# Last block of transposes without the output projection woven in (three causal layers), and four pairs of the mixed layer in two groups

## Chip, cores and metric

The kernel runs on one core of one Trainium2 chip. The metric is the device time of one execution in microseconds (us), from the start of the program to its end. A profiled execution also has a span, from its first to its last instruction.

## What is computed

Four layers of one block (MLA, sliding window "SWA", forgetting attention "FOX", MLA again), then one "mixed" layer with attention over heads of two kinds, a gated feed-forward part and a last gated projection. One sequence of 512 tokens, width 1024, everything in float32. Cut to what matters here:

```python
def first_block(x, ...):
    for i in range(DEPTH):                      # MLA, SWA, FOX, MLA
        y = branch(x)                           # (o * silu(gate)) @ w_out, o = causal softmax attention, 16 heads
        x = _layernorm(DEEPNORM_ALPHA * x + y, ln_g[i], ln_b[i])
    return x

def second_block(x, ...):
        z = rmsnorm(x, g_mix_pre[i]) @ w_in[i]
        ya = short_conv_mixer(a_in, a_c, a_b, conv_w[i])
        yb = pool_mixer(pv, pool_w[i], pool_scale[i])
        yc = dsa_mixer(...)                     # 4 heads, 128 keys of each query chosen by top-k, bias by distance
        yd = moba_mixer(...)                    # 4 heads, all past keys, bias by distance
        mix = jnp.concatenate([ya, yb, yc, yd], axis=-1) @ w_out[i]
        x = x + rmsnorm(mix, g_mix_post[i])
        f = swiglu(rmsnorm(x, g_ffn_pre[i]), w_gate_up[i], w_down[i])
        ...
```

## The kernel before

Every engine runs a program written out by hand, and semaphores tie them together. TensorE (PE) does all products. A float32 product is made of three fp32r products (high by high, high by low, low by high), so each weight that SyncE's queue brings in is split: ScalarE (ACT) copies the high part (`w_hi`, L1465), GpSimd (POOL) subtracts to get the low part (`w_lo`, L2992). A "unit" is one such weight piece. A **tile** is 24 matmuls of 128x512 for one unit of 128 columns (L545); its result lands in one of two PSUM banks, 6 and 7, ACT copies the high part out (L1494) and VectorE (DVE) the low part (L2182), which frees the bank. `three` (L496 to L498) is the same trick for the other products, the output projection `w_out` among them: one k-step of it has 24 matmuls, 6 for each of four rows of tokens.

Attention runs on **pairs** of heads. For a pair PE makes scores in three chunks (L735; for the chosen keys a further product L752 adds the mask of the top-k), DVE adds the bias and takes the maximum (L2334, "maxima"), ACT takes the exponential (L1596, "exps"), the result is divided by the sum, PE turns it by 20 transposes (L781, in 6 **turns** of 4, 4 and 2), ACT copies each turn out of PSUM (L1630), and PE multiplies by the values (L798, "mix", 16 matmuls).

In the causal layers (MLA, FOX, MLA) the division is DVE's (L2363), and the eight pairs go in four groups of two: `fill` (tiles and values for the next group), then a **block** of 12 turns on six banks, two mixes, and the scores of the next two pairs. The last group is different. `last_block` first calls `ahead(0)`, the first k-step of the output projection for two of its four rows, and then weaves two turns at a time between the products of `ahead(0)` to `ahead(2)`, 36 matmuls in all, and its turns have only two banks (4 and 5), since the projection holds 0 to 3:

```python
                    ahead(0)
                    two()
                    woven.append(each_second)
                    ahead(1)
                    ahead(2)
                    woven.pop()
                    while todo:
                        two()
```

In the mixed layer there are four pairs: 0 and 1 over all past keys, 2 and 3 over chosen keys. They are not grouped: `step` interleaves the turns of pair i with the scores of pair i+2, two banks for the turns, and tiles of queries and keys stand between them. Here ACT does the division (L1611), and DVE finds the chosen keys by 16 rounds of MAX8 and MATCH_REPLACE8 for each row of queries (L2803, L2804, `top`). The values of pairs 2 and 3 are made in two halves (L627), one before `mix(1)` and one before `mix(2)`, and ACT copies each half out (L1517). `mixed_ahead` then weaves the turns of pair 3 into the output projection.

## Time and profile before

| what | us |
|---|---|
| median of 3 runs | 1645.56 (1645.0 to 1646.14) |
| the profiled execution, its own time | 1647.99 |
| its span | 1645.8 |
| PE busy | 1626.4, 99% |
| DVE busy | 778.5, 47% |
| ACT busy | 763.9, 46% |

The span is 2.2 us below the profiled execution's own time, and within 0.3 us of the median of the runs. Times of day below are us from the start of the span. Matmuls overlap, so the time that a piece of PE's work takes is read from the start of its first instruction to the start of the next piece, not from the busy column.

### The profile page before, as it was taken

To read this page: it belongs to the slowest core of one execution; us is meant where nothing else is said; L and a number is where in the kernel's file an instruction comes from. 1 tells how busy PE (TensorE), PEld (TensorE's weight loads), DVE (VectorE), ACT (ScalarE), POOL (GpSimd) and SP (SyncE) were. 2 spreads that over 40 slices of the span, in tenths; PEclk is the share of its full clock that TensorE was granted. 3 is DMA by queue.
4 is the path that set the end of the run, shared out by engine and by line. 5 is a ranking of instruction groups with operands and counts; after the bars stand their busy time and mean duration, and the time that the engine had idled before them with its cause. 6 is when DMAs were issued, how large, how long until landed. Compare 5 with 4: busy or idle time off the path is not lost.

```text
span 1645.8 us, 24549 instructions
## 1 busy us (share of the span) xinstructions
PE 1626.4 (99%) x9349; PEld 1345.9 (82%) x9349; DVE 778.5 (47%) x2048; ACT 763.9 (46%) x1565; POOL 657.1 (40%) x551
## 2 busy tenths in 40 slices
PE   8999999999999999999999999999999999999998
PEld 8787879888888888778878788787788888888877
DVE  2787735665554433445878556896051111001152
ACT  4477634565344534633667534338553322212252
POOL 4423234332344224134333144882335444444423
PEclk9999999999999999999999999999999999999999
DMA  6322244323443223144232066241243333333312
GB/s 175 74 44 66 73 154 133 82 69 73 155 141 99 67 77 90 39 167 116 51 69 83 29 195 190 60 115 52 93 126 106 100 92 100 103 91 102 120 60 90
DMA packets 216048, 161.19 MB, mean 98 GB/s; under 512 B 53755, under 2 KB 197147, under 8 KB 215932
## 3 DMA queue, kind: packets, MB, share of 16 engines
q1 hardware_dynamic: 205904, 130.21, 28.1%
q10 hardware_dynamic: 9804, 29.38, 5.6%
q8 instruction: 75, 1.23, 0.3%
q14 instruction: 41, 0.34, 0.1%
q0 software_dynamic: 224, 0.03, 0.1%
HBM read 148.32 MB, written 11.14 MB: 97 GB/s over the span
## 4 chain that ended last, share of the span: by engine, by line
PE 88%; DVE 7%; ACT 2%; issue 1%; DMA 0%; ACTq 0%; POOL 0%; DVEq 0%; SPq 0%
PE banks L545 44%; PE banks L496 8%; PE banks L498 8%; PE banks L497 8%; PE banks L781 5%; PE banks L798 4%; PE banks L627 4%; PE banks L735 4%; PE banks L758 1%; DVE banks L2486 1%; DVE banks L2475 1%; DVE AB L2488 1%; ACT G L1743 1%; PE banks L1009 1%; DVE AB L2334 1%
## 5 line engine op out<-in xcount | busy, mean ns | idle before, releaser
L2992 POOL TENSOR_TENSOR w_lo<-w_raw,w_hi 128x512 fp32r<-128x512 f32 (+2 forms) x506 | 616.4, 1245 | 958.7 <-ACT w_hi L1465 947.7
L1465 ACT ACTIVATE w_hi<-w_raw 128x1024 fp32r<-128x1024 f32 (+4 forms) x254 | 250.2, 995 | 179.2 <-PE banks L498 107.2
L545 PE MATMUL banks<-XTh,w_hi 128*128 128x512 f32 (+5 forms) x1216 | 277.6, 370 | 1.7 <-DVE XTl L2448 1.4
L545 PE MATMUL banks<-XTl,w_hi 128*128 128x512 f32 (+5 forms) x1216 | 270.8, 365 | 0.0
L545 PE MATMUL banks<-XTh,w_lo 128*128 128x512 f32 (+5 forms) x1216 | 270.7, 365 | 0.0
L545 PEld LDWEIGHTS banks<-XTh,w_hi 128*128 128x128 f32 (+2 forms) x1216 | 208.2, 187 | 47.7 <-issue 8.2
L545 PEld LDWEIGHTS banks<-XTl,w_hi 128*128 128x128 f32 (+2 forms) x1216 | 211.0, 187 | 37.7
L545 PEld LDWEIGHTS banks<-XTh,w_lo 128*128 128x128 f32 (+2 forms) x1216 | 211.0, 187 | 37.4
L1596 ACT ACTIVATE AB<-AB,nb 128x256 f32<-128x256 f32 (+3 forms) x288 | 152.6, 533 | 37.7 <-DVE nb L2344 32.4
L496 PE MATMUL banks<-w_hi,OTh 128*128 128x512 f32 (+1 forms) x432 | 166.7, 386 | 0.3
L498 PE MATMUL banks<-w_hi,OTl 128*128 128x512 f32 (+1 forms) x432 | 162.4, 376 | 0.0
L497 PE MATMUL banks<-w_lo,OTh 128*128 128x512 f32 (+1 forms) x432 | 162.2, 375 | 0.0
L2363 DVE TENSOR_SCALAR_CACHE_REDUCE AB<-AB,ri 128x256 f32<-128x256 f32 (+3 forms) x256 | 118.2, 518 | 2.3
L1630 ACT ACTIVATE AB<-banks 128x512 f32<-128x512 f32 (+1 forms) x200 | 89.9, 566 | 37.0 <-PE banks L781 36.6
L2182 DVE TENSOR_TENSOR QKl<-banks,QKh 128x512 fp32r<-128x512 f32 (+2 forms) x80 | 54.6, 683 | 110.8 <-ACT QKh L1494 110.6
L2883 DVE TENSOR_TENSOR otmp<-banks,AB 128x512 f32<-128x512 f32 x22 | 15.2, 692 | 192.1 <-PE banks L545 192.1
L496 PEld LDWEIGHTS banks<-w_hi,OTh 128*128 128x128 f32 x432 | 81.7, 189 | 18.8 <-DVE QKl L2182 2.4
L498 PEld LDWEIGHTS banks<-w_hi,OTl 128*128 128x128 f32 x432 | 81.7, 189 | 15.0
L497 PEld LDWEIGHTS banks<-w_lo,OTh 128*128 128x128 f32 x432 | 81.7, 189 | 13.2
L1494 ACT ACTIVATE QKh<-banks 128x512 fp32r<-128x512 f32 (+2 forms) x80 | 46.9, 587 | 91.1 <-PE banks L545 67.3
L2334 DVE CUSTOM_DVE_ANT_0 AB<-banks,zmask 128x256 f32<-128x256 f32 (+1 forms) x192 | 81.5, 487 | 7.5 <-PE banks L758 5.2
L781 PE MATMUL banks<-ident,AB 128*128 128x128 f32 x672 | 83.2, 274 | 0.8
(232 smaller groups left out, 2265.6 us busy)
## 6 DMA issues: line engine op xcount, KB each, us to landing
w_raw<-in_w_gate_up_dram SPq DMA_DIRECT2D x44, 512.0 KB, 3.7
w_raw<-in_fox_w_in_dram SPq DMA_DIRECT2D x30, 512.0 KB, 4.1
w_raw<-in_mla_w_in_dram SPq DMA_DIRECT2D x26, 512.0 KB, 4.5
w_raw<-in_w_in_dram SPq DMA_DIRECT2D x24, 512.0 KB, 3.9
w_raw<-in_w_down_dram SPq DMA_DIRECT2D x22, 512.0 KB, 3.5
w_raw<-in_swa_w_in_dram SPq DMA_DIRECT2D x20, 512.0 KB, 4.0
w_raw<-in_mla_w_out_dram SPq DMA_DIRECT2D x16, 512.0 KB, 3.6
x_spill<-AB ACTq DMA_DIRECT2D x16, 512.0 KB, 2.8
```

The costliest lines, as they stand in the source:

```text
L496: nc.tensor.matmul(o, ah, bh, start=first, stop=False, skip_group_check=True)
L497: nc.tensor.matmul(o, ah, bl, start=False, stop=False, skip_group_check=True)
L498: return nc.tensor.matmul(o, al, bh, start=False, stop=last, skip_group_check=True)
L545: mm = nc.tensor.matmul(o, wt[:, k, :], xt[:, k, lo:hi], start=first and n == 0 and k == 0, stop=last and n == 2 and k == nk - 1, skip_gro ...
L627: mm = nc.tensor.matmul(o[:, 256 * (t % 2):256 * (t % 2) + 256], xt[:, k, ts], parts[k // 4][low][:, k % 4, :], start=n == 0 and k == 0, s ...
L781: mm = nc.tensor.transpose(turn_bank(m, grouped or six, block_at[1])[:, o:o + P], SBP[a % 2][x][:, col:col + P], ident[:, :])
L1465: nc.scalar.activation(view(w_hi, u, RING), view(w_raw, u, RAW), ACT.Copy).then_inc(hi_done, 1)
L1596: ins = nc.scalar.activation(sc, sc, ACT.Exp, bias=nb[:, b, n0 + t:n0 + t + 1], scale=pr.scale, accum_out=rs[:, b, n0 + t:n0 + t + 1])
L1630: nc.scalar.activation(dst[:, pr.pt[js[0]]:pr.pt[js[0]] + width], src[:, 0:width], ACT.Copy).then_inc(pt_free, 1)
L2334: ins = nc.vector.tensor_tensor_reduce(pr.score(b, x, t), o, pr.bias(t, x), 1.0, -3e38, ALU.add, ALU.max, mx[:, b, 4 * x + t:4 * x + t + 1])
L2363: ins = nc.vector.tensor_scalar(pr.score(b, x, t), pr.score(b, x, t), ri[:, b, 4 * x + t:4 * x + t + 1], None, ALU.mult, ALU.add, accum_ou ...
L2992: ins = pool.tensor_tensor(low[at], raw[at], high[at].bitcast(F32), ALU.subtract)
```

## The change

In the causal layers `pair_attention` is called with no `ahead`: all four groups run the same loop, the last one too, with its block of 12 turns on six banks, its two mixes, and then the whole output projection (`pairs=True` keeps its waits on single pairs). In the mixed layer the pairs become grouped: PE's order is the same loop as in the causal layers, and ACT and DVE get a new `scaled_groups`. SWA keeps `last_block`.

```diff
@@ PE, groups()
-                        last = s == n_pairs // 2 - 1
+                        last = s == n_pairs // 2 - 1 and ahead is not None
                         fill(s)
                         if last:
                             last_block(s)
...
-                        if not last:
-                            for i in (2 * s + 2, 2 * s + 3):
-                                for ch in range(s_len):
-                                    scores(i, ch)
+                        for i in (2 * s + 2, 2 * s + 3):
+                            for ch in range(s_len):
+                                scores(i, ch)
@@ PE, the three causal layers
-                pair_attention(mla_pairs(), fill, lambda k: out_ahead("out", src, k, each=True))
-                out_rows("out", KD, src, turned=(lambda t: HT[t % 2]) if j else (lambda t: x_tok[:, t, :]), 
+                pair_attention(mla_pairs(), fill, None)
+                out_rows("out", KD, src, pairs=True, turned=(lambda t: HT[t % 2]) if j else (lambda t: x_tok[:, t, :]), 
...
@@ PE, mixed layer
+            def fill(s):
+                if s < 0:
+                    pair_tile("q", 1)
+                    pooled(1)
+                    mark["mixed_g"] = c.g
+                    pair_tile("k", 1)
+                    pe.wait_ge(pool_out, 2)
+                elif s == 0:
+                    for p in (2, 3):
+                        pair_tile("q", p)
+                        pair_tile("k", p)
+                else:
+                    parts.extend([unit("v"), unit("v")])
+                    for half in range(2):
+                        value_half(parts, half)
...
+                    ready_pv[c.pair + 2] = c.g
@@ ACT
+                def scaled_groups():
+
+                    fill(-1, 0)
+                    for s in range(n_pairs // 2):
+                        for k in range(2):
+                            i = 2 * s + k
+                            exps(i, 0)
+                            exps(i, 1)
+                            fill(s, 2 * k)
+                            norm(i, 0)
+                            norm(i, 1)
+                            fill(s, 2 * k + 1)
+                        block_at[0] = c.tch
+                        turned(2 * s)
+                        turned(2 * s + 1)
+                        store(2 * s)
+                        store(2 * s + 1)
...
+                elif s == 0:
+                    pair_tile(2 + pos // 2 + pos % 2 * 4)
                 elif pos == 1:
-                    if i < 1:
-                        pair_tile(i + 7)
-                    elif i == 1:
-                        advance()
-                        values(0)
-                    elif i == 2:
-                        values(1)
-                elif pos == 5 and i == 2:
                     advance()
-
-            pair_attention(rel_pairs(), fill, (2,))
+                    values(0)
+                elif pos == 2:
+                    values(1)
+                    advance()
@@ DVE
+            def fill(s, pos):
+                if s < 0:
+                    top(3)
+                    pair_tile(1)
+                    pooled(1)
+                    top(2)
+                    pair_tile(5)
+                elif s == 0:
+                    pair_tile(2 + pos // 2 + pos % 2 * 4)
+                    top((3, 1, 3, 48)[pos])
```

Three places show the order. First PE at the end of the first MLA layer's attention, before the change: the last of the woven pieces (L496 to L498 the projection, L781 transposes, L798 the mixes).

```order
L781 MATMUL banks<-ident,AB 128x128 x8
L496 MATMUL banks<-w_hi,OTh 128x512
L497 MATMUL banks<-w_lo,OTh 128x512
L498 MATMUL banks<-w_hi,OTl 128x512
L496 MATMUL banks<-w_hi,OTh 128x512
L497 MATMUL banks<-w_lo,OTh 128x512
L498 MATMUL banks<-w_hi,OTl 128x512
L781 MATMUL banks<-ident,AB 128x128 x12
L798 MATMUL banks<-AB,V_odd 64x512 x2
```

The same place after the change, from the last gate tile (L545) on:

```order
L545 MATMUL banks<-XTl,w_hi 128x512 x8
L545 MATMUL banks<-XTh,w_lo 128x512 x8
L781 MATMUL banks<-ident,AB 128x128 x40
L798 MATMUL banks<-AB,V_odd 64x512 x2
L798 MATMUL banks<-AB,V_odd 64x384 x2
```

The 36 matmuls of the projection that stood before and between the transposes have moved behind the mixes.

Second, PE in the mixed layer before the change, at the end of pair 0's first two chunks of scores (L735), where the key tile of pair 1 follows:

```order
L735 MATMUL banks<-QKh 128x512 x2
L735 MATMUL banks<-QKl,QKh 128x512 x2
L735 MATMUL banks<-QKh,QKl 128x512 x2
L545 MATMUL banks<-XTh,w_hi 128x512 x8
L545 MATMUL banks<-XTl,w_hi 128x512 x8
```

and after it, where pair 0's last chunk of scores is followed by pair 1's first two:

```order
L735 MATMUL banks<-QKh 128x512 x2
L735 MATMUL banks<-QKl,QKh 128x512 x2
L735 MATMUL banks<-QKh,QKl 128x512 x2
L735 MATMUL banks<-QKh 128x256 x2
L735 MATMUL banks<-QKl,QKh 128x256 x2
L735 MATMUL banks<-QKh,QKl 128x256 x2
L735 MATMUL banks<-QKh 128x384 x2
```

The six chunks of pairs 0 and 1 now follow each other, and the four tiles of pairs 2 and 3 come behind them.

Third, ACT ahead of the turns of the mixed layer's second group, after the change (L1509 a half of the values, L1457 a weight split, L1603 the division, L1622 the copies of turns):

```order
L1509 ACTIVATE V<-banks 128x512
L1457 ACTIVATE w_hi<-w_raw 128x1024
L1603 ACTIVATE AB<-AB,ri 128x128
L1603 ACTIVATE AB<-AB,ri 128x256
L1603 ACTIVATE AB<-AB,ri 128x384
L1603 ACTIVATE AB<-AB,ri 128x512
L1603 ACTIVATE AB<-AB,ri 128x128
L1603 ACTIVATE AB<-AB,ri 128x256
L1603 ACTIVATE AB<-AB,ri 128x384
L1603 ACTIVATE AB<-AB,ri 128x512
L1622 ACTIVATE AB<-banks 128x512 x2
```

and before it (L1630 the copies, L1465 the split, L1611 the division):

```order
L1630 ACTIVATE AB<-banks 128x512 x2
L1630 ACTIVATE AB<-banks 128x256
L1465 ACTIVATE w_hi<-w_raw 128x1024
L1611 ACTIVATE AB<-AB,ri 128x128
L1611 ACTIVATE AB<-AB,ri 128x256
```

The first copy of pair 2's turns stood ahead of pair 3's division, and stands behind the whole of it now.

## Rows read from the trace of the kernel before

**Rows 1.** The page: span and the engines' busy time.

```profile
span 1645.8 us, 24549 instructions
PE 1626.4 (99%) x9349; PEld 1345.9 (82%) x9349; DVE 778.5 (47%) x2048; ACT 763.9 (46%) x1565; POOL 657.1 (40%) x551
```

**Rows 2.** Timeline of PE, first MLA layer, last group: start, length, line, operation, count.

```profile
196.82 0.39 PE L496 MATMUL banks<-w_hi,OTh 128*128 128x512 f32 x1
199.55 1.03 PE L781 MATMUL banks<-ident,AB 128*128 128x128 f32 x8
...
210.09 4.53 PE L798 MATMUL banks<-AB,V_odd 128*64 128x512 f32 x32
214.55 0.50 PE L496 MATMUL banks<-w_hi,OTh 128*128 128x512 f32 x1
```

**Rows 3.** Timeline of PE, the same layer's third group: block and mixes.

```profile
170.28 4.53 PE L781 MATMUL banks<-ident,AB 128*128 128x128 f32 x40
174.74 4.53 PE L798 MATMUL banks<-AB,V 128*64 128x512 f32 x32
```

**Rows 4.** Timeline of DVE, what follows the last division, MLA and FOX.

```profile
199.56 0.68 DVE L2215 SCALAR_TENSOR_TENSOR G<-G,banks 128x512 f32<-128x512 f32 x1
...
689.05 0.68 DVE L2215 SCALAR_TENSOR_TENSOR G<-G,banks 128x512 f32<-128x512 f32 x1
```

**Rows 5.** Timeline of PE, FOX, last group: start of the projection.

```profile
685.86 0.39 PE L496 MATMUL banks<-w_hi,OTh 128*128 128x512 f32 x1
```

**Rows 6.** Timeline of PE, mixed layer.

```profile
1088.43 2.00 PE L545 MATMUL banks<-XTh,w_hi 128*128 128x512 f32 x8
...
1093.90 1.02 PE L1269 MATMUL banks<-AB 128*128 128x512 f32 x2
...
1108.52 0.44 PE L735 MATMUL banks<-QKh 64*128 64x384 f32 x2
...
1110.28 2.11 PE L545 MATMUL banks<-XTh,w_hi 128*128 128x512 f32 x8
...
1154.02 1.20 PE L627 MATMUL banks<-w_hi,XTh 128*128 128x256 f32 x8
...
1159.94 1.72 PE L798 MATMUL banks<-AB,V 128*64 128x512 f32 x8
1163.51 0.87 PE L798 MATMUL banks<-AB,V 128*64 128x256 f32 x8 [1.84 <-ACT V L1517]
...
1178.91 0.50 PE L496 MATMUL banks<-w_hi,OTh 128*128 128x512 f32 x1
```

**Rows 7.** Stretches: length, busy of PE, PEld, DVE, ACT, POOL, granted clock, DMA.

```profile
170.30:174.70 4.40, 4.40 (x41) 4.28 (x39) 4.29 (x15) 4.22 (x11) 2.30 (x2) 1.00 0.57 183
1164.58:1167.98 3.40, 3.40 (x9) 2.63 (x9) 0.69 (x1) 1.17 (x3) 0.00 (x0) 0.50 0.51 154
```

**Rows 8.** Timeline of PE, start of the mixed layer: its next longest wait.

```profile
996.26 1.11 PE L545 MATMUL banks<-XTh,w_hi 128*128 128x128 f32 x8 [0.97 <-DVE XTl L2448]
```

**Rows 9.** Timeline of DVE, mixed layer: one round of the top-k and the next.

```profile
1091.46 0.69 DVE L2803 MAX8 top<-misc 128x8 f32<-128x512 f32 x1
...
1092.97 0.69 DVE L2803 MAX8 top<-misc 128x8 f32<-128x512 f32 x1
```

**Rows 10.** Stretches of one line: length, busy: DVE L2334, then ACT L1596, ACT L1630.

```profile
1111.70:1119.90 8.20, 3.43 (x16) 1.00 0.00 0
1152.50:1156.88 4.38, 4.36 (x16) 1.00 0.02 4
170.90:176.20 5.30, 5.13 (x12) 1.00 0.60 201
```

**Rows 11.** Timeline of ACT, mixed layer: weight split, division, half of the values.

```profile
1160.11 1.06 ACT L1465 ACTIVATE w_hi<-w_raw 128x1024 fp32r<-128x1024 f32 x1 [0.66 <-PE banks L627]
1161.07 1.90 ACT L1611 ACTIVATE AB<-AB,ri 128x128 f32<-128x128 f32 x4
1162.88 0.57 ACT L1517 ACTIVATE V<-banks 128x512 f32<-128x512 f32 x1
```

More of the change, by code:

```diff
@@ L458, in rel_pairs @@
                          lambda t, x, p=p: G[:, (2 * p + x + 4) % 8, S - CAUSAL_KEYS[t]:S],
-                         (OTh, OTl, (6, 7, 4, 5)[p]), sel=p >= 2, grouped=False) for p in range(4)]
+                         (OTh, OTl, (6, 7, 4, 5)[p]), sel=p >= 2) for p in range(4)]
         SEL = [None, misc[:, 0:256], misc[:, 256:640], misc[:, 640:1152]]
@@ L941, in out_ahead, with out_rows @@
                             weave()
-            def out_rows(name, n, src, first=True, last=True, turned=None, turn_at=None, chunk_at=None, early=None):
-                paired = bool(begun)
-                if not begun and not chunk_at:
+            def out_rows(name, n, src, first=True, last=True, turned=None, turn_at=None, chunk_at=None, early=None, pairs=False):
+                paired = pairs or bool(begun)
+                if not paired and not chunk_at:
                     groups_stored(pe, c.g)
@@ L1229, in src @@
                 return OTh[:, FOX_OUT[k], ts], OTl[:, FOX_OUT[k], ts]
-            pair_attention(fox_pairs(), fill, lambda k: out_ahead("out", src, k, each=True))
-            out_rows("out", KD, src, turned=lambda t: x_tok[:, t, :], turn_at=TURNS["ln"], early=early_ln("c", "c", "c"))
+            pair_attention(fox_pairs(), fill, None)
+            out_rows("out", KD, src, pairs=True, turned=lambda t: x_tok[:, t, :], turn_at=TURNS["ln"], early=early_ln("c", "c", "c"))
             mla(1)
@@ L1320, in _ @@
             pe.wait_ge(idx_r, 24)
[L1321 removed]
+            pair_attention(rel_pairs(), fill, None)
+            pe.wait_ge(conv_lo, 2)
             out_rows("out", KD, src, turned=lambda t: HT[t % 2], turn_at=TURNS["rms"], chunk_at=chunk_at, early=early_ff)
@@ L1617, in turned @@
                     pr = pairs[i]
-                    last = i >= n_pairs - 2
+                    last = i >= n_pairs - 2 and pr.window
                     for x in range(2):
@@ L1666, in pair_attention @@
                 if grouped:
-                    groups()
+                    if pairs[0].gate is None:
+                        scaled_groups()
+                    else:
+                        groups()
                     c.pair += n_pairs
@@ L2390, in gated_low, with scaled_groups @@
                     low_part(i, otmp[:, :]).then_inc(po_lo, 1)
+                def scaled_groups():
+                    fill(-1, 0)
+                    for i in range(2):
+                        for ch in range(s_len):
+                            maxima(i, ch)
+                    for s in range(n_pairs // 2):
+                        i = 2 * s
+                        norm(i, 0)
+                        norm(i, 1)
+                        fill(s, 0)
+                        fill(s, 1)
+                        norm(i + 1, 0)
+                        norm(i + 1, 1)
+                        fill(s, 2)
+                        fill(s, 3)
+                        mixed(i)
+                        for ch in range(s_len):
+                            maxima(i + 2, ch)
+                        mixed(i + 1)
+                        for ch in range(s_len):
+                            maxima(i + 3, ch)
                 def groups():
@@ L2421, in groups @@
                             maxima(i + 3, ch)
-                if grouped:
+                if pairs[0].gate is None:
+                    scaled_groups()
+                elif grouped:
                     groups()
@@ L2855, in _, with fill @@
             dve.wait_ge(x_out, 16 * T * 4)
-            def fill(i, pos):
-                if pos == 0:
-                    if i < 0:
-                        top(3)
-                    if i < 1:
-                        pair_tile(i + 3)
-                        if i == -2:
-                            pooled(1)
-                elif pos == 1:
-                    if i < 0:
-                        top(2)
-                    if i < 1:
-                        pair_tile(i + 7)
-                    elif i < 3:
-                        c.g += 1
-                elif pos == 3 and i == -1:
-                    top(48)
+            def fill(s, pos):
+                if s < 0:
+                    top(3)
+                    pair_tile(1)
+                    pooled(1)
+                    top(2)
+                    pair_tile(5)
+                elif s == 0:
+                    pair_tile(2 + pos // 2 + pos % 2 * 4)
+                    top((3, 1, 3, 48)[pos])
+                elif pos == 0:
+                    c.g += 2
             pair_attention(rel_pairs(), fill)
```

40 lines of the change are left out of this document (5 added, 35 removed).

## The prediction, made before the changed kernel had run

> **What bounds the kernel now.** I read the page first: PE is busy for 1626.4 of 1645.8 us, DVE and ACT for less than half [rows 1]. So only what shortens PE's own work, or the waits in it, can shorten the kernel. PE's waits come next, and they are short: in the list of waits the longest that the change can touch is one of 1.84 us on ACT's copy of a value half, in the mixed layer [rows 6]. Then the timeline of PE at the two places that the change rewrites, and last the timelines of DVE and ACT there, to see whether they can feed the new order. The sum is made against the span of 1645.8 us, which is 0.24 us above the median of the runs.
>
> **Causal layers (MLA, FOX, MLA).** In the last group of the first MLA layer, PE takes 214.55 - 196.82 = 17.73 us from the first product of the projection to the first one behind the mixes [rows 2]: 36 products, 40 transposes, 32 mix matmuls. The parts apart: the 12 products ahead of the first turn take 199.55 - 196.82 = 2.73 us, 0.2275 each [rows 2], and I take 0.2285 for one in a long run, so 36 take 8.23. A block of 40 transposes on six banks takes 174.74 - 170.28 = 4.46 us, and the mixes behind it 214.55 - 210.09 = 4.46 [rows 2, 3]. The sum is 17.15, so weaving costs 0.58 us over doing the pieces apart: the two-bank turns at its end wait for ACT's copies, and each change between products and transposes costs a little. FOX starts its last group at 685.86 [rows 5] and has the same interval, and so has the second MLA layer. Gain: 3 x 0.58 = 1.74 us.
>
> This holds if nothing has to be waited for. What covered the last division before was the projection. Now the block starts at 196.82, and needs the last pair's second head for its last ten transposes, 3/4 of 4.46 later, at 200.17. DVE has it at 199.56 [rows 4]. In FOX the block would start at 685.86 [rows 5] and need it at 689.2; DVE has it at 689.05 [rows 4]. So the cover is 0.6 us in MLA and 0.15 in FOX; if DVE came 0.5 us later, FOX alone would lose 0.35. The mixes' results are needed only by the fourth row of the first k-step, 18 products or 4.1 us behind them, and DVE takes them off in less, so the 36 products behind the mixes cost their 8.23 us and nothing more. No DMA is issued earlier or later relative to the rows of the projection that use it. From both sides: no gain (the two banks' waits come back elsewhere) to 1.74; I take 1.74.
>
> **Mixed layer.** Before, PE takes 1178.91 - 1088.43 = 90.48 us from the query tile of pair 1 to behind the last mix [rows 6]; without the 36 products woven in (8.23) it is 82.25. Walked through in the new order, with its prices: a tile 5.47 us (1088.43 to 1093.90), pooling about 1, two chunks of scores 1.76 (1108.52 to 1110.28) [rows 6], all three 2.3; for chosen keys the added mask makes a pair 4.0; a block 4.46 and two mixes 4.46 [rows 3]; one value half 5.9 (1154.02 to 1159.94) [rows 6], both in a row 11.65, since one switch falls away. That is 5.5 + 1.0 + 5.6 + 4.6 + 22.2 + 8.9 + 8.0 + 11.65 + 8.9 = 76.4 us of work, 5.9 less than 82.25. Two new waits eat it.
>
> First wait, scores of pairs 0 and 1. PE reaches them at 1100.5. DVE is on the top-k: from 1091.46 on a round takes 1.51 us [rows 9], five rounds and the pooling end at 1102.4, and only then comes the low part of pair 1's key, to 1103.0, and the first maximum. One pair's maxima take 3.43 us [rows 10], and PE may run only three chunks ahead. So PE does pair 0 until 1102.8, waits 1.0, does a chunk, waits 0.85, does another, waits 0.3, and ends at 1107.25: 2.15 us of waiting. Before, tiles stood between the chunks and hid DVE. Between 0 (DVE earlier) and 3.4 (a whole pair's maxima bare), I take 2.15.
>
> Then four tiles to 1129.5 (ACT splits and both stores keep up), block and mixes to 1138.4, the chosen pairs' scores to 1146.45. They need the last mask. Four rounds of the top-k are left behind the last key tile's store at 1130.8, so DVE has it at 1137.2, and PE asks for it at 1140.9: 3.7 us of cover. The value halves end at 1158.1.
>
> Second wait, the block of pairs 2 and 3. ACT has pair 2's maxima at 1144.0 and then, in its order: exps of pair 2, 4.4 [rows 10]; division, 2 x 1.81 (1161.07 to 1162.88); split 0.95; value half 0.5 [rows 11]; exps of pair 3, 4.4; the second value half, which PE ends at 1158.1; another split; division of pair 3, 3.6. That ends at 1163.3, and only then does ACT copy the first turn. PE does pair 2's six turns by 1160.3, fills its six banks and stands for 3.6 us. From 1163.9 it follows ACT's copies, 12 in about 4.9 us [rows 10], to the last mix, which ends at 1170.8. Without waiting it would be 1167.0: 3.8 us lost. Between 0 and 5, I take 3.8.
>
> So the layer's part ends at 1170.8 against 1088.43 + 82.25 = 1170.7: +0.1. The gain of fewer switches and of the old wait is given back.
>
> **The clock.** Before, PE stands for 1.84 us before 1163.51 [rows 6]; the granted clock then is 0.50 (1.2 GHz) from 1164.58 to 1167.98 [rows 7], with PE full, which costs half of 3.4: 1.7 us. A wait of 0.97 us [rows 8] is followed by no such stretch. The new wait of 3.6 us should be followed by one too, and part of it falls on transposes that wait for ACT anyway: 1.4 instead of 1.7, -0.3. The first wait, 2.15 us in three pieces within 4.5, may or may not bring another, +1.7.
>
> The blocks themselves: while PE does nothing but transposes from 170.30 to 174.70, the granted clock is 1.00 [rows 7]. The Trainium skill speaks against this change there ("TensorE: Matmul & The Clock Gate", section "Part 4: PE-mode transpose"): transposes do not count as PE being busy in the way that matmuls do. By it the new blocks would bring down the clock, by the row they don't; the sum goes by the row.
>
> **Sum.** 1645.8 - 1.74 + 0.1 - 0.3 = 1643.9 us.
>
> **Rivals.**
> (a) The same, and the first wait brings the clock down as well: +1.7, 1645.6. For it: its pieces add up to more than the 1.84 us that did it; against it, they are apart.
> (b) Slower. The long runs of transposes bring the clock down: five new blocks (three last groups, two in the mixed layer), each followed by a stretch as the one of half clock in [rows 7], 1.7 us apiece: 1643.9 + 8.5 = 1652.4. It decides from the third such block (-1.9 + 5.1 = +3.2). The nine blocks of 40 that stand in the trace already speak against it.
> (c) Faster. One or both new waits fail to appear, since DVE and ACT keep up: 1.84 us of idle and 1.7 of clock are gone and nothing replaces them. Without the second wait, 1643.9 - 3.8 - 1.4 = 1638.7; with only half of both waits and no fallen clock, 1643.9 - 3.0 - 1.4 = 1639.5. Against it is ACT's order, in which pair 2's copies stand behind pair 3's division.
> (d) Nothing comes of the causal layers, because DVE's last division or the first copy is late: 1645.6, as before.
> (e) The second wait is longer, and the clock falls for two stretches instead of one, with (a) on top: 1643.9 + 1.7 + 1.7 = 1647.3, slower by 0.1%. It needs 3.4 us more than my sum to leave the band.
>
> **Chances.** Forecast 0.42, (a) 0.25, (b) 0.03, (c) 0.13, (d) 0.07, (e) 0.10. A measurement of this kernel tells some 0.2%, 3.3 us, from no change. Faster by more: (c) and a little of the forecast's own spread, 0.16. Slower by more: (b) and the far end of (e), 0.07. Within: 0.77. Low end 1641.0, where a good half of the second wait is missing; high end 1647.6, beyond (e). Between them lie all but (b) and most of (c).
>
> **What would show each step.** Causal layers: 12.69 us, not 13.27, from the end of the last gate tile to the mixes plus the 36 products; one stretch of 40 transposes in 4.46 us, and no wait of L781 on DVE. Mixed layer: waits of the scores on DVE of about 2 us before the four tiles; one wait of transposes on ACT of 3 to 4 us with pair 2's turns ahead of it and the first copy behind pair 3's division; no wait of the scores on the top-k; a stretch of granted clock 0.50 behind the long wait. I am wrong if the second wait is absent, if it exceeds 5 us, or if the clock falls beside a block that nothing interrupts.

## The result: slower by 0.25%, outside the predicted range

| what | before | after |
|---|---|---|
| median us (20 executions each) | 1645.86 (1645.0 to 1648.5) | 1650.73 (1646.43 to 1656.76) |
| ratio after to before, 95% interval | | 1.0025 (1.0019 to 1.0032) |
| span of the profiled execution | 1645.8 | 1648.6 |
| its own time | 1647.99 | 1650.41 |
| mean granted clock of that span | 0.999 | 0.996 |

The forecast was 1643.9 with a range up to 1647.6. By the medians the change costs 4.9 us where a gain of 1.9 was forecast. The ratio with its interval, 0.25% or 4.1 us, is not the quotient of the two medians: the executions of before stand in two groups some 2 us apart, and a median does not see the upper one.

The 20 executions of the changed kernel show already what a longer time goes with. The one at a mean granted clock of 0.999 took 1646.43 us, three at 0.997 took 1647.36 to 1648.66, fifteen at 0.996 took 1650.27 to 1651.65, and one at 0.992 took 1656.76.

### The profile page after: what moved, and what is told of

Same layout as the page of the kernel before. It is cut to its first block, busy times and chain, and to the rows that moved or that the text cites. A ratio compares the mean times of both kernels' runs of the same rounds, so it can differ in the third digit from the quotient of the medians.

```text
span 1648.6 us, 24514 instructions
## 1 busy us (share of the span) xinstructions
PE 1625.8 (99%) x9349; PEld 1350.5 (82%) x9349; DVE 779.3 (47%) x2048; ACT 762.7 (46%) x1565; POOL 657.9 (40%) x551
## 4 chain that ended last, share of the span: by engine, by line
PE 86%; DVE 9%; ACT 2%; issue 1%; DMA 1%; ACTq 0%; POOL 0%; DVEq 0%; SPq 0%
PE banks L545 43%; PE banks L496 8%; PE banks L498 8%; PE banks L497 8%; PE banks L798 5%; PE banks L781 5%; PE banks L735 4%; PE banks L627 4%; PE banks L758 1%; DVE banks L2519 1%; DVE banks L2508 1%; DVE AB L2521 1%; PE banks L1008 1%; ACT G L1755 1%; DVE misc L2837 1%
## 5 line engine op out<-in xcount | busy, mean ns | idle before, releaser
L1457 ACT ACTIVATE w_hi<-w_raw 128x1024 fp32r<-128x1024 f32 (+4 forms) x254 | 251.2, 997 | 211.7 <-PE banks L498 150.3
L545 PE MATMUL banks<-XTh,w_hi 128*128 128x512 f32 (+5 forms) x1216 | 278.2, 371 | 1.7 <-DVE XTl L2481 1.4
L545 PE MATMUL banks<-XTh,w_lo 128*128 128x512 f32 (+5 forms) x1216 | 271.5, 366 | 0.0
L545 PE MATMUL banks<-XTl,w_hi 128*128 128x512 f32 (+5 forms) x1216 | 270.8, 365 | 0.0
L545 PEld LDWEIGHTS banks<-XTh,w_hi 128*128 128x128 f32 (+2 forms) x1216 | 209.2, 188 | 48.1 <-issue 8.6
L545 PEld LDWEIGHTS banks<-XTh,w_lo 128*128 128x128 f32 (+2 forms) x1216 | 211.8, 188 | 37.3
L545 PEld LDWEIGHTS banks<-XTl,w_hi 128*128 128x128 f32 (+2 forms) x1216 | 211.0, 187 | 37.6
L496 PE MATMUL banks<-w_hi,OTh 128*128 128x512 f32 (+1 forms) x432 | 164.3, 380 | 0.4
L498 PE MATMUL banks<-w_hi,OTl 128*128 128x512 f32 (+1 forms) x432 | 161.5, 374 | 0.0
L496 PEld LDWEIGHTS banks<-w_hi,OTh 128*128 128x128 f32 x432 | 81.2, 188 | 18.9 <-DVE QKl L2191 2.4
L498 PEld LDWEIGHTS banks<-w_hi,OTl 128*128 128x128 f32 x432 | 81.3, 188 | 14.6
L497 PEld LDWEIGHTS banks<-w_lo,OTh 128*128 128x128 f32 x432 | 81.4, 188 | 13.6
L1622 ACT ACTIVATE AB<-banks 128x512 f32<-128x512 f32 (+1 forms) x200 | 86.7, 580 | 5.8 <-PE banks L781 5.8
L781 PE MATMUL banks<-ident,AB 128*128 128x128 f32 x672 | 80.4, 277 | 3.7 <-ACT AB L1622 3.6
```

The lines of the kernel that those rows point to most:

```text
L496: nc.tensor.matmul(o, ah, bh, start=first, stop=False, skip_group_check=True)
L497: nc.tensor.matmul(o, ah, bl, start=False, stop=False, skip_group_check=True)
L498: return nc.tensor.matmul(o, al, bh, start=False, stop=last, skip_group_check=True)
L545: mm = nc.tensor.matmul(o, wt[:, k, :], xt[:, k, lo:hi], start=first and n == 0 and k == 0, stop=last and n == 2 and k == nk - 1, skip_gro ...
L781: mm = nc.tensor.transpose(turn_bank(m, grouped or six, block_at[1])[:, o:o + P], SBP[a % 2][x][:, col:col + P], ident[:, :])
L1457: nc.scalar.activation(view(w_hi, u, RING), view(w_raw, u, RAW), ACT.Copy).then_inc(hi_done, 1)
```

## The profile after the change

The page, the rows that answer to [rows 1]:

```profile
span 1648.6 us, 24514 instructions
PE 1625.8 (99%) x9349; PEld 1350.5 (82%) x9349; DVE 779.3 (47%) x2048; ACT 762.7 (46%) x1565; POOL 657.9 (40%) x551
```

The timeline of PE at the end of the first MLA layer's attention, then FOX (start, length, what, count), to lay beside [rows 2, 5]:

```profile
196.23 4.53 PE L781 MATMUL banks<-ident,AB 128*128 128x128 f32 x40
200.69 4.53 PE L798 MATMUL banks<-AB,V_odd 128*64 128x512 f32 x32
205.15 0.50 PE L496 MATMUL banks<-w_hi,OTh 128*128 128x512 f32 x1
...
684.61 4.67 PE L781 MATMUL banks<-ident,AB 128*128 128x128 f32 x40
689.21 4.53 PE L798 MATMUL banks<-AB,V_odd 128*64 128x512 f32 x32
```

The block takes 200.69 - 196.23 = 4.46 us and the mixes 4.46, as forecast; in FOX the block takes 4.60. DVE is done with the last division at 199.02, 0.6 us before it is needed. What comes after the last division in MLA, to lay beside [rows 4]:

```profile
199.02 0.68 DVE L2224 SCALAR_TENSOR_TENSOR G<-G,banks 128x512 f32<-128x512 f32 x1
```

The mixed layer, timeline of PE: the first query tile, the two waits of the scores on DVE, the tiles behind them, the first block, the chosen pairs' values, the second block with its wait on ACT, the mixes, the projection.

```profile
1087.74 2.00 PE L545 MATMUL banks<-XTh,w_hi 128*128 128x512 f32 x8
...
1103.27 0.38 PE L735 MATMUL banks<-QKh 64*128 64x256 f32 x2 [1.43 <-DVE mx L2343]
...
1104.55 0.44 PE L735 MATMUL banks<-QKh 64*128 64x384 f32 x2 [0.67 <-DVE mx L2343]
...
1107.35 2.61 PE L545 MATMUL banks<-XTh,w_hi 128*128 128x512 f32 x8
...
1129.77 4.53 PE L781 MATMUL banks<-ident,AB 128*128 128x128 f32 x40
...
1146.78 1.10 PE L627 MATMUL banks<-w_hi,XTh 128*128 128x256 f32 x8
...
1158.28 2.35 PE L781 MATMUL banks<-ident,AB 128*128 128x128 f32 x20
1164.26 4.50 PE L781 MATMUL banks<-ident,AB 128*128 128x128 f32 x20 [3.64 <-ACT AB L1622]
1168.69 5.09 PE L798 MATMUL banks<-AB,V 128*64 128x512 f32 x32
1173.71 0.50 PE L496 MATMUL banks<-w_hi,OTh 128*128 128x512 f32 x1
```

ACT at the second wait: pair 3's eight divisions, and only behind them the copies of the turns:

```profile
1159.92 3.72 ACT L1603 ACTIVATE AB<-AB,ri 128x128 f32<-128x128 f32 x8
1163.54 3.82 ACT L1622 ACTIVATE AB<-banks 128x512 f32<-128x512 f32 x9
```

Both waits are where they were forecast: 1.43 + 0.67 us against 2.15 (the third piece, forecast at 0.3, is not seen here, and is 0.14 us in three of the traces below), and 3.64 against 3.6. What differs is TensorE's clock. Stretches of the same trace (length, then busy of PE, PEld, DVE, ACT, POOL, granted clock, DMA): three of half clock, and the first block for comparison.

```profile
995.81:999.20 3.39, 3.39 (x19) 3.39 (x18) 0.11 (x1) 0.60 (x1) 0.00 (x0) 0.50 0.00 0
1105.03:1108.43 3.40, 3.40 (x19) 2.46 (x16) 3.37 (x19) 2.47 (x9) 0.00 (x0) 0.50 0.00 0
1163.06:1169.87 6.81, 5.61 (x24) 4.66 (x26) 0.00 (x0) 5.77 (x13) 0.00 (x0) 0.50 0.27 77
1129.80:1134.20 4.40, 4.40 (x41) 4.26 (x39) 4.23 (x10) 4.40 (x12) 2.53 (x2) 1.00 0.27 88
```

13.6 us at 1.2 GHz stand in the mixed layer, against 3.4 in [rows 7]. One of these stretches comes right behind the wait of 0.98 us at the layer's start. The change does not touch this wait, and the trace of before has no such stretch behind it [rows 7, 8].

## The experiments

To compare, the mixed layer is measured from the first turns in the projection ahead of it to the first turns in its own projection. Here is how that interval is read, timeline of PE of the kernel after: 1210.62 - 975.03 = 235.6 us.

```profile
975.03 0.82 PE L1008 MATMUL banks<-ident,AB 128*128 128x128 f32 x6
...
1210.62 0.93 PE L1008 MATMUL banks<-ident,AB 128*128 128x128 f32 x7
```

All kernels, each median beside that of before on the same chip. The last two columns are of the profiled execution alone, the half-clock time being what the granted clock at 0.50 covers inside the interval.

| kernel | median us | before there | ratio, 95% interval | mixed interval | at half clock |
|---|---|---|---|---|---|
| before, in [rows 7] | 1645.86 | | | 230.5 | 3.4 |
| before again | 1645.56 (one) | 1645.44 | | 228.8 | 0 |
| after | 1650.73 | 1645.86 | 1.0025 (1.0019 to 1.0032) | 235.6 | 13.6 |
| after again | 1649.06 (one) | 1645.44 | | 234.4 | 10.2 |
| causal part only | 1645.12 | 1645.9 | 1.0000 (0.9990 to 1.0009) | 230.4 | 3.4 |
| mixed part only | 1650.63 | 1645.9 | 1.0028 (1.0017 to 1.0040) | 234.5 | 10.2 |
| both waits filled | 1646.37 | 1645.9 | 1.0003 (0.9994 to 1.0011) | 231.9 | 3.4 |
| first wait filled | 1648.22 | 1646.21 | 1.0003 (0.9994 to 1.0012) | 233.0 | 6.8 |
| second wait filled | 1648.08 | 1646.21 | 1.0004 (0.9995 to 1.0012) | 233.3 | 6.8 |
| DVE divides (2, 3) | 1642.91 | 1645.9 | 0.9978 (0.9969 to 0.9987) | 229.6 | 6.8 |
| both waits off | 1641.24 | 1645.44 | 0.9968 (0.9955 to 0.9980) | 225.7 | 0 |
| best: DVE divides (1 to 3) | 1639.16 | 1646.21 | 0.9952 (0.9940 to 0.9965) | 225.6 | 3.4 |
| top-k later | 1641.21 | 1646.21 | 0.9960 (0.9947 to 0.9972) | 225.4 | 0 |
| before, its wait filled | 1645.56 | 1645.44 | 0.9996 (0.9987 to 1.0005) | 228.8 | 0 |

A median can jump by 2 us when one or two executions change their group, so small differences of medians are read with care below, and beside the intervals inside a trace.

My theory after the result: the waits are those I forecast, and the loss comes from the clock that falls behind them, in more places and for longer than I had booked. The rivals: the long runs of transposes, or the grouped order itself, cost the time, and the clock is a bystander.

### The causal part alone

```diff
 (kernel before)
-                        last = s == n_pairs // 2 - 1
+                        last = s == n_pairs // 2 - 1 and ahead is not None
...
-                pair_attention(mla_pairs(), fill, lambda k: out_ahead("out", src, k, each=True))
+                pair_attention(mla_pairs(), fill, None)
```

> The kernel before with the causal part of the change alone: the mixed layer stays ungrouped. Clock theory (the loss comes from the mixed layer's new waits, behind which the granted clock falls): the three last groups save 0.58 us each, nothing else moves, so 1.7 us less than before, some 1644.1 against 1645.86, ratio 0.9990, granted clock 0.999 as before. Rival (the long runs of nothing but transposes bring the clock down in most executions, and the profiled one did not show it): each of three new blocks may cost 1.7 us, so 1645.8 to 1649, and a granted clock under 0.999.

Measured: 1645.12 against 1645.9, and by the interval of the ratio no difference can be told. The gain is seen inside the trace: the layers that end with a last group take 289.35 us (FOX) and 247.11 us (second MLA), against 289.93 and 247.76 in the trace of before, 0.58 and 0.65 less. In the first MLA layer the last group shows it: from its first instruction to the 38th product of the projection it takes 213.71 - 196.23 = 17.48 us in the changed kernel and 214.88 - 196.82 = 18.06 before, 0.58 less. The clock does not fall in any of the three layers. The rival (blocks of transposes) is gone. The term of 1.74 stands by these intervals, while the medians show 0.8; the interval of the ratio reaches from 1.6 us less to 1.5 more, so the runs of this kernel do not confirm the 1.74 by themselves.

### The mixed part alone

```diff
 (kernel after)
-            pair_attention(mla_pairs(), fill, None)
+            pair_attention(mla_pairs(), fill, lambda k: out_ahead("out", src, k, each=True))
```

> The changed kernel with the causal layers put back (projection woven into the last block). Clock theory: the whole loss is in the mixed layer, so 1.7 us more than the changed kernel, some 1652.4, granted clock 0.996 as after the change. Rival (the causal layers' blocks share in the loss): less than 1650.7.

Measured: 1650.63, so the whole loss is in the mixed layer. The 1.7 us more did not come. The clock fell for less time here, which makes up for it: 10.2 us in the profiled execution and not 13.6, and a mean granted clock of 0.997 in five of six executions, against 0.996 in most of after's. Laid beside the second profile of after (below), which has the same 10.2 us at half clock, this span is 1.3 us longer (1648.5 against 1647.2). The clock's spread is as large as the causal part.

### Both waits filled: the clock apart from the wait

```diff
+                    if pairs[0].gate is None and i == 1:
+                        keep_busy((6, 3, 0)[ch])
...
+                def keep_busy(n):
+                    o = begin()
+                    for _ in range(n):
+                        nc.tensor.matmul(o[:, :], QKh[:, 0, 0:P], QKh[:, 0, :], start=True, stop=True, skip_group_check=True)
...
+                                if pairs[0].gate is None and (i, x, ch) == (3, 0, 0):
+                                    keep_busy(15)
```

> The changed kernel, with matmuls of no use (their results are overwritten) put in front of the mixed layer's two waits: 6 and 3 ahead of the second pair's first two chunks of scores, 15 ahead of the transposes that wait for ACT; at 0.23 us each they fill 1.4, 0.7 and 3.4 us. The waits' ends are set by DVE and ACT as before, so PE gains no time by them. Clock theory: PE is busy, the clock stays at 1.00 around 1103 and 1164, and three of the four half-clock stretches of 3.41 us go: 3 x 1.7 = 5.1 us less than the changed kernel, some 1645.6, granted clock 0.999. Rival (the wait itself or the grouped order is what costs, the clock falls for another reason): no gain, 1650.7 within 0.5.

Measured: 1646.37, 4.4 us less than after. Timeline of PE from the query tile of pair 1 and at the first block, then at the second wait (L768 are the added matmuls, L788 the transposes, L805 the mixes):

```profile
1087.54 2.00 PE L545 MATMUL banks<-XTh,w_hi 128*128 128x512 f32 x8
...
1128.46 4.53 PE L788 MATMUL banks<-ident,AB 128*128 128x128 f32 x40
...
1156.97 2.35 PE L788 MATMUL banks<-ident,AB 128*128 128x128 f32 x20
1159.07 3.67 PE L768 MATMUL banks<-QKh 128*128 128x512 f32 x15
1162.95 2.58 PE L788 MATMUL banks<-ident,AB 128*128 128x128 f32 x20 [0.21 <-ACT AB L1631]
1165.46 4.53 PE L805 MATMUL banks<-AB,V 128*64 128x512 f32 x32
1169.92 0.50 PE L496 MATMUL banks<-w_hi,OTh 128*128 128x512 f32 x1
```

Stretches of the same trace around the two places:

```profile
1101.50:1106.50 5.00, 5.00 (x35) 3.43 (x33) 4.93 (x24) 0.75 (x3) 0.00 (x0) 1.00 0.37 107
1157.00:1169.90 12.90, 12.69 (x89) 9.04 (x87) 0.87 (x2) 10.77 (x24) 2.56 (x2) 1.00 0.17 62
```

PE still has to wait for ACT until 1162.95. From the first transposes to the end of the wait it is 1162.95 - 1156.97 = 5.98 us, as in after (1164.26 - 1158.28), so the wait ends no earlier; but the 20 transposes behind it take 2.5 us instead of 4.4 and the mixes 4.46 instead of 5.02. From the first transposes of the block to the projection it is 12.95 us against 15.43. Work of no use made the kernel 4.4 us faster by the medians (3.6 by the ratios, 1.0025 and 1.0003), with the second wait's end where it was. So this much of the loss is the clock and not the wait.

### Each wait filled by itself

The diff is the same, with only the first or only the second `keep_busy`.

> The changed kernel with matmuls of no use ahead of the first wait only (6 and 3, as in the run that filled both); the second wait of 3.63 us stays bare. Clock theory: the stretch near 1105 goes, those behind the second wait stay; that stretch cost 1.1 us in the first profile after the change and more in the second, where it was twice as long: some 1649.2 against 1650.73. Rival (one wait alone decides for both places): either all goes (1646.4) or nothing (1650.7).

> The changed kernel with 15 matmuls of no use ahead of the second wait only; the first waits of 1.4 and 0.7 us stay bare. Clock theory: the stretches behind 1164 go, worth 2.8 us in the first profile after the change, the one near 1105 stays: some 1648.0. Rival as in the run before: 1646.4 or 1650.7.

Measured: 1648.22 and 1648.08, that is 2.5 and 2.65 less than after, 5.2 together; both at once gave 4.4. My 1649.2 for the first was a microsecond too high. The medians alone do not separate these kernels from the one with both waits filled: the ratios to before are 1.0003, 1.0004 and 1.0003 with intervals that cover each other, and before was itself 0.35 us slower on this chip. What decides are the traces, one of each. The stretch at the filled place is gone and the one at the bare place stands, so the places act each for itself, and neither decides for the other. Stretches at the two places with the first wait filled:

```profile
1101.00:1108.00 7.00, 6.98 (x43) 5.06 (x42) 6.96 (x34) 3.18 (x13) 0.00 (x0) 1.00 0.28 76
1161.23:1168.03 6.80, 6.02 (x24) 4.66 (x26) 0.00 (x0) 5.35 (x13) 0.00 (x0) 0.50 0.27 77
```

and with the second wait filled:

```profile
1105.92:1109.31 3.39, 3.25 (x12) 2.16 (x11) 3.35 (x19) 3.01 (x12) 0.00 (x0) 0.50 0.00 0
1157.00:1171.00 14.00, 13.79 (x96) 10.49 (x97) 0.71 (x2) 12.65 (x31) 2.56 (x2) 1.00 0.26 76
```

### Both kernels profiled again

> The kernel before, unchanged, for a second profile. The prediction took its span of 1645.8 as typical, though that execution's own time (1647.99) is 2.1 us over the median. Expected: a typical execution has a span near 1643.7, the stretch behind the 1.84 us wait, no stretch behind the 0.97 us wait at the layer's start, and the difference of 2.1 us shows at one place in the intervals between the layers' ends.

> The changed kernel, unchanged, for a second profile. Clock theory: the waits of 1.4, 0.7 and 3.6 us stand at the same places with the same lengths, and half-clock stretches behind both; whether one also follows the 0.98 us wait at the layer's start is open (it did in four traces with the grouped mixed layer, and in neither of the two with the ungrouped one). If the places of the stretches differ and the time differs by 1.7 us for each, the chip's clock is the reason for the spread between executions.

Measured: spans 1643.7 and 1647.2. Timeline of PE of before again, at the layer's first turns, at the query tile of pair 1, and at its wait in the mixed layer:

```profile
977.00 0.81 PE L1009 MATMUL banks<-ident,AB 128*128 128x128 f32 x6
...
1087.98 2.00 PE L545 MATMUL banks<-XTh,w_hi 128*128 128x512 f32 x8
...
1163.04 0.87 PE L798 MATMUL banks<-AB,V 128*64 128x256 f32 x8 [1.84 <-ACT V L1517]
```

and the stretch behind it:

```profile
1164.20:1167.60 3.40, 3.40 (x21) 2.89 (x20) 0.69 (x1) 1.34 (x3) 0.00 (x0) 1.00 0.49 154
```

The same wait of 1.84 us as in [rows 6], and behind it the full clock, where I had expected the stretch to stand again: the mixed interval is 228.8 us, 1.6 less than in the trace that I had predicted from. It is the only change between the layers' ends of the two traces but for 0.5 us in the first layer, where the start differs: 16 transposes at the program's start take 3.04 us in the first trace and 2.52 in this one, with the same code. And stretches of after again, behind the wait at the layer's start, and at the first and second wait:

```profile
993.90:997.30 3.40, 3.40 (x31) 3.40 (x32) 1.45 (x2) 0.27 (x2) 0.00 (x0) 1.00 0.00 0
1102.57:1109.37 6.80, 6.51 (x26) 5.09 (x27) 5.48 (x30) 5.10 (x17) 0.00 (x0) 0.50 0.00 1
1164.01:1167.40 3.39, 3.39 (x16) 3.39 (x17) 0.00 (x0) 3.23 (x9) 0.00 (x0) 0.50 0.32 127
```

Nothing stands behind the start's wait this time, but the first wait (1.42 and 0.66 us) has twice the length at half clock, and the second (3.63 us) half of it. The waits repeat to 0.02 us; what the clock does behind them does not.

### The wait of before filled

```diff
 (kernel before, mix)
+                    if a in ready_pv_late:
+                        keep_busy(o, 8)
                     for j in range(T):
                         if j == 2 and a in ready_pv_late:
```

> The kernel before, with eight matmuls of no use (1.8 us, results overwritten) in front of the first value product of pair 2, so that PE is busy while ACT copies the value half out; the value half's arrival is unchanged. If the half-clock stretch behind that wait stands in most executions of before, its 1.7 us go: 1644.2 against 1645.9. If it was only in the profiled execution, nothing changes: 1645.9 within 0.4.

Measured: 1645.56 against 1645.44, no change of the median. But in that series 6 of 15 executions of before lay between 1646.96 and 1647.86, a group of their own, and of this kernel one of 11 (1647.21). So a fallen clock behind the 1.84 us wait may be the reason for before's upper group, and the profile that I predicted from, at 1647.99, was one of it. This is not shown: 6 of 15 against 1 of 11 is little, a stretch behind the wait at the layer's start would cost as much, and the trace of the causal part alone has the stretch behind the 1.84 us wait, though that execution, at 1644.95, lies below its kernel's median.

### The waits taken away

DVE divides for pairs 2 and 3, so that ACT can copy at once:

```diff
 (ACT, norm)
-                    if not 0 <= i < n_pairs or pairs[i].gate is not None:
+                    if not 0 <= i < n_pairs or pairs[i].gate is not None or pairs[i].sel:
 (DVE, norm)
-                    if pr.gate is None:
+                    if pr.gate is None and not pr.sel:
```

> The changed kernel, with the division of the mixed layer's pairs 2 and 3 done by DVE instead of ACT, so that ACT can copy the turns as soon as PE has made them. Both theories: the second wait of 3.64 us goes. Clock theory: with it go its two half-clock stretches, 3.4 us, together 7.0 less: some 1643.7. Rival (the clock falls with the block of transposes or for another reason): 3.6 less, 1647.1, with the half-clock stretch still there around the block. A third possibility is that DVE's division of pair 3 is late by about 1 us, since eight divisions of a pair take it 4.1 us; then a wait of transposes on DVE shows.

Measured: 1642.91, 7.8 us less than after. The block takes 4.90 us and the mixes 4.45, with no wait and at full clock, so both the 3.6 us and its clock are gone, and the block of 40 transposes is still there (timeline of PE):

```profile
1158.40 4.96 PE L781 MATMUL banks<-ident,AB 128*128 128x128 f32 x40
1163.30 4.53 PE L798 MATMUL banks<-AB,V 128*64 128x512 f32 x32
1167.75 0.50 PE L496 MATMUL banks<-w_hi,OTh 128*128 128x512 f32 x1
```

The stretch of block and mixes:

```profile
1158.40:1167.75 9.35, 9.32 (x74) 6.36 (x72) 2.30 (x8) 7.15 (x15) 2.50 (x2) 1.00 0.20 56
```

Then the first wait too, by the query tile of pair 2 between the scores of pairs 0 and 1 (PE's order alone changes), here called both waits off:

```diff
                     for i in range(2):
                         for ch in range(s_len):
                             scores(i, ch)
+                        if i == 0 and pairs[0].gate is None:
+                            fill(-2)
...
+                if s == -2:
+                    pair_tile("q", 2)
```

> The changed kernel with both new waits taken away: DVE divides for pairs 2 and 3 as in the run before, and on TensorE the query tile of pair 2 stands between the scores of pair 0 and those of pair 1, so that DVE catches up behind it. Clock theory: against the run in which DVE alone divides (1642.91) the first wait of 2.1 us goes and with it its half-clock stretch, worth 1.1 us there: some 1639.7, granted clock 0.999, and no stretch of half clock between 1100 and 1170. Rival (the clock falls in the grouped layer whatever PE waits for): 2.1 less at most, 1640.8, with a stretch still there near 1105.

Measured: 1641.24, less gain than forecast, because ACT, which gets pair 1's scores later now, is late for the first block. The time is nearer to the rival's 1640.8 than to my 1639.7; the trace, of one execution, speaks for the clock theory, with no stretch of half clock anywhere in the mixed layer. Timeline of PE:

```profile
1125.13 2.34 PE L781 MATMUL banks<-ident,AB 128*128 128x128 f32 x20
1128.73 2.56 PE L781 MATMUL banks<-ident,AB 128*128 128x128 f32 x20 [1.26 <-ACT AB L1626]
```

A stall was moved, not removed, and the way to see it beforehand is the same as in the prediction: add up what stands on ACT between the last maximum and the first copy. The next kernel, the best, takes pair 1's division off ACT as well and puts two rounds of the top-k into DVE's idle time (`fill(-2, 0)` is `top(1)` there):

```diff
 (ACT, norm; PE's order as in both waits off)
-                    if not 0 <= i < n_pairs or pairs[i].gate is not None:
+                    if not 0 <= i < n_pairs or pairs[i].gate is not None or i:
...
 (DVE)
                             maxima(i, ch)
+                        if i == 0:
+                            fill(-2, 0)
...
-                    top((3, 1, 3, 48)[pos])
+                    top((3, 2, 2, 48)[pos])
```

> The kernel with both waits off had a new wait: 1.26 us for ACT's first copy of the first block, since ACT has pair 1's exponentials and division right before it. Here DVE divides for pair 1 too, and two of its rounds of the top-k move into its idle time (one behind pair 0's maxima, one ahead of pair 1's division). Expected: the 1.26 us go, no stretch of half clock from 1090 to 1170, the mixed layer's interval 224.4, the whole some 1640.0 against 1641.24 of both waits off and about 1645.6 of before. Rival: DVE's last mask now comes late, since the division costs it 3.9 us and its idle time gives back 3.4; then the scores of pair 2 wait for DVE by up to 1 us.

Measured: 1639.16, against 1646.21 of before, the lowest median of all; the interval of its ratio overlaps those of both waits off and of top-k later. The first block runs through, and the product that adds the last mask does not wait (no brackets behind L752); the rival is out:

```profile
1126.66 4.53 PE L781 MATMUL banks<-ident,AB 128*128 128x128 f32 x40
1131.12 4.53 PE L798 MATMUL banks<-AB,V_odd 128*64 128x512 f32 x32
...
1137.56 0.62 PE L752 MATMUL banks<-OTh,ident_r 128*128 128x384 f32 x2
```

Two stretches of it, the first behind the wait at the layer's start:

```profile
997.32:1000.71 3.39, 3.39 (x19) 3.39 (x17) 1.51 (x3) 2.04 (x4) 0.00 (x0) 0.50 0.19 76
1090.00:1170.00 80.00, 79.97 (x512) 63.79 (x511) 60.97 (x193) 48.98 (x120) 28.01 (x23) 1.00 0.26 79
```

From 1090 to 1170 PE is busy for 79.97 of 80.00 us at full clock. Its profiled execution has the stretch behind the wait at the layer's start, 1.7 us, and took 1641.05; three of the five executions took 1638.32 to 1639.16.

Last, shorter waits instead of none: DVE divides for pairs 2 and 3, and two rounds of the top-k stand behind the scores instead of ahead of pair 1's key.

```diff
 (DVE, fill)
                     pooled(1)
-                    top(2)
                     pair_tile(5)
```

> The changed kernel with DVE dividing for pairs 2 and 3 (no second wait), and with two rounds of the top-k moved from ahead of the store of pair 1's key to behind the scores, instead of a tile between the scores. Expected: the first waits shrink from 2.2 to 1.4 us in pieces of 0.3 to 0.6, the mask still in time. Clock theory: shorter waits bring the clock down in fewer executions or none: some 1641 against 1642.91, with the mean granted clock 0.999. Rival (any wait there brings it down): 1642.0, a stretch near 1105 as before.

Measured: 1641.21. The waits are 0.14, 0.67 and 0.15 us (0.96, against 1.4 forecast); the longest, in PE's timeline:

```profile
1101.25 0.44 PE L735 MATMUL banks<-QKh 64*128 64x384 f32 x2 [0.67 <-DVE mx L2343]
```

and in this execution the clock stays at full around them:

```profile
1096.00:1110.00 14.00, 13.05 (x85) 10.17 (x84) 8.93 (x41) 8.72 (x23) 4.62 (x5) 1.00 0.32 95
```

The profiled execution is the fastest of the five, 1639.74. Three of the others took 1641.21 to 1641.62 with a mean granted clock of 0.998, against 1.000 in the two at 1639.8. So in most executions the clock did fall somewhere, and whether it fell behind these waits is not shown. The run does not decide between the theory and its rival.

## Why the prediction was wrong

**Causal layers, -1.74: right by the traces.** The block stands in 4.46 us as forecast; the first MLA layer's last group gives 0.58 us, and FOX and the second MLA layer give 0.58 and 0.65 us in the kernel with this part alone, 0.51 and 0.60 in the changed one.

**Mixed layer, the walk through PE's work: right.** From pair 1's query tile to the projection I had forecast 1088.43 to 1170.8, 82.37 us at full clock. Where the clock did not fall behind either wait (both filled), it is 1169.92 - 1087.54 = 82.38, and the changed kernel without what its fallen clock adds is 85.97 - 1.1 - 2.5 = 82.4 (the two amounts are worked out below). The two waits have the lengths (to 0.05 us), the places and the causes that were named.

**The clock, -0.3: wrong, and this is the step that failed.** Three errors are in it.

1. Bookkeeping. The 82.25 us that I compared the walk with came from a trace in which nine of the 36 projection products ran wholly or in part at half clock [rows 7] (the first 12 take 4.44 us from start to start, 2.87 in before again), and I took the 36 out at their full-clock price. So some 1.6 us of fallen clock were still in the 82.25, and none in the 82.37. "1.4 instead of 1.7, -0.3" should have been "+1.4 beside +0.1". With my own numbers the sum is 1645.8 - 1.74 + 0.1 + 1.4 = 1645.6, no gain at all.
2. The base. I took the trace's span, 1645.8, as typical since it lay near the median. But a span must be laid beside spans: that execution's own time was 1647.99, 2.1 us over the median, and before again has 1643.7. Filling before's wait left its median where it was, so most executions of before have no fallen clock behind it; at full clock its interval is 228.8 us, and that of the changed one 231.9 - 1.7 = 230.2 (the filled kernel, without the stretch at the layer's start). The mixed part is a loss of 1.4 us before the clock counts, and the causal part's 1.74 less 1.4 leaves -0.3. The added matmuls of the first wait run over by some 0.2 us (1104.60 - 1087.54 = 17.06 us from the query tile to the second late chunk, against 1104.55 - 1087.74 = 16.81 in the changed kernel), so the 1.4 may be that much too high and the 1.1 below that much too low; that 82.38 meets 82.37 so exactly is luck.
3. The size of the clock's term. In the changed kernel's trace the three places cost 112.71 - 110.98 = 1.7 us (from the layer's first turns to the query tile of pair 1, against before again), 42.03 - 40.92 = 1.1 (from there to the first block) and 15.43 - 12.95 = 2.5 (from the second block to the projection), the last two against the kernel with both waits filled. Together 5.3 us; with -0.3 that is 5.0, and the medians differ by 4.9. I had allowed 1.4 for one place. But the 1.7 at the layer's start are not the change's doing: the kernel with the mixed part only has this stretch too, and every engine's instructions up to there and 50 us beyond are those of before. So of the change's own this trace shows 1.1 + 2.5 - 0.3 = 3.3 us, and after again, which has no stretch at the start, is 3.5 us longer than before again (spans 1647.2 and 1643.7). That 5.0 meets 4.9 so well is in part chance; which stretches make up the rest in the other executions was not traced.

**The rivals.** (a) named the first wait's stretch and gave it 0.25; in all five traces with that wait bare, the clock fell there. (e), a second wait with two stretches on top of (a), is what the profiled execution shows, at 0.10 and 1647.3, though the wait was not longer than forecast. Both were priced on top of a sum that was 1.7 us too low, and so was the range's upper end, which lies 3.7 us above that sum and not 3.4 as (e) has it. (b), the blocks of transposes, fell with the causal part alone and with DVE's division: the blocks of 40 stay and the clock stays at full beside them. In no trace did the clock fall between 1090 and 1170 without one of the new waits, or before's of 1.84 us, in front of it. (c) needed DVE or ACT to keep up, and they did only when the work was moved. (d) did not occur.

What stays open: why the medians of the causal part alone show 0.8 us where its intervals give 1.7, and why a wait that repeats to 0.1 us has a fallen clock behind it for twice as long in one execution as in the next, or (the waits of 0.98 and 1.84 us) not at all.

## What to carry to other kernels

Where PE is busy 99% of the time, a wait costs its own length and then whatever half-clock time follows it, and the second part can be the larger: the 2.1 us of the first wait brought 1.1 us more in one profile of after and 2.5 in the other. So count new waits as chances of a fallen clock, and before comparing a walk with a measured interval take the half-clock stretches out of both. And lay the profiled execution's own time beside the median of the runs before its span is used as a base: if it is 2 us off, a stretch in it may be the exception.

## What was not expected of the hardware

A wait's length did not decide whether the clock falls. The wait of 0.97 or 0.98 us at the mixed layer's start stands in all 14 traces; a stretch at 1.2 GHz follows it in six (after, mixed part only, both filled, second filled, DVE divides, best) and not in the other eight. The wait of 1.84 us was followed by one in two traces of three. The first wait, 1.4 and 0.7 us, was followed by one or two in five of five, the second, 3.63 us, in four of four; 1.26 us (both waits off) and 0.67 us (top-k later) by none in the one trace of each.

The Trainium skill says in "TensorE: Matmul & The Clock Gate", section "Part 1: The HAM clock gate (the "warmup" mystery)", that the chip's watch over TensorE's activity runs on by itself and does not start anew with the kernel. The traces agree in that the clock falls behind the same wait, with the same work around it, in some executions and not in others; no run here shows the mechanism itself.

What a fallen clock costs depends on what PE does in it: 1.6 us for 3.4 with products of 512 columns (before and before again), but 2.5 us for the 6.8 from 1163.05 on, since 1.2 of them passed in the wait itself and the transposes behind it follow ACT in part.
